# Storing the two fp32r parts of x column-block-major for the expert gather's weight loads

## The reference, cut to what matters

```python
x = layer_norm(ALPHA * x + h, ln1_g[i], ln1_b[i])
m = moe_ffn(x, router_w[i], router_bias[i], exp_w1[i], exp_w3[i], exp_w2[i], sh_w1[i], sh_w3[i], sh_w2[i])
x = layer_norm(ALPHA * x + m, ln2_g[i], ln2_b[i])
...
def step(out, args):            # one expert, inside moe_ffn
    tok, g, e = args
    xe = xpad[tok]              # the tokens of this expert: the gather
    h = jax.nn.silu(xe @ w1[e]) * (xe @ w3[e])
    y = (h @ w2[e]) * g[:, None].astype(xe.dtype)
    return out.at[tok].add(y), None
```

## Time and profile before

| | us |
|---|---|
| median of 3 runs | 1493.35 (1493.33 to 1494.79) |
| the profiled execution | 1495.15 |
| its span in the profile | 1493.4 |
| PE busy | 1432.8 (96%) |
| PEld busy | 900.3 (60%) |
| DVE, ACT, POOL busy | 508.3, 356.5, 50.2 |
| share of the chain that ended last | PE 91%, DVE 5%, ACT 2% |
| HBM traffic | 308 GB/s over the span, 400 to 420 GB/s in the expert loops |

### The profile page before, as it was taken

The page is one execution under the profiler, slowest core; times in us unless marked ns, Lnnn a source line. Parts: engine busy times, 40 slices in busy tenths (PEclk is TensorE's granted clock), DMA queues, the critical chain, the costliest instruction groups (busy, mean ns, idle before and its releaser), DMA issues.

```text
span 1493.4 us, 21684 instructions
## 1 busy us (share of the span) xinstructions
PE 1432.8 (96%) x8704; PEld 900.3 (60%) x8704; DVE 508.3 (34%) x840; ACT 356.5 (24%) x878; POOL 50.2 (3%) x75
## 2 busy tenths in 40 slices
PE   8978999999999999999899999999999999999988
PEld 3467586566565656654478476765666656565543
DVE  0397261332323223232610346222323322232253
ACT  1137132222222222221210242222222222222211
POOL 1220010000000000000100001000000000000000
PEclk9969999999999999999899999999999999999999
DMA  9530147999999999998564504499999999999951
GB/s 308 181 148 1 74 178 322 400 416 407 413 414 412 411 405 414 408 418 343 166 213 145 225 2 169 174 420 411 400 409 414 410 421 405 413 404 409 421 211 56
DMA packets 80807, 461.89 MB, mean 309 GB/s; under 512 B 9168, under 2 KB 9392, under 8 KB 30544
## 3 DMA queue, kind: packets, MB, share of 16 engines
q1 hardware_dynamic: 78128, 452.07, 75.1%
q0 software_dynamic: 2592, 8.53, 1.9%
HBM read 459.52 MB, written 1.05 MB: 308 GB/s over the span
## 4 chain that ended last, share of the span: by engine, by line
PE 91%; DVE 5%; ACT 2%; issue 1%; DMA 0%; SPq 0%; DVEq 0%
PE ps L907 30%; PE ps L935 15%; PE ps L877 10%; PE ps L949 9%; PE ps L1053 4%; PE ps L794 4%; PE ps L749 3%; PE ps L634 3%; PE ps L766 2%; PE ps L818 2%; PE ps L590 1%; PE ps L917 1%; PE ps L619 1%; PE ps L513 1%; PE ps L734 1%; PE ps L827 1%
## 5 line engine op out<-in xcount | busy, mean ns | idle before, releaser
L1681 DVE TENSOR_TENSOR o_tok<-ps,o_tok 128x1024 f32<-128x1024 f32 x128 | 156.6, 1224 | 347.0 <-PE ps L949 347.0
L935 PE MATMUL ps<-ring,qkT 128*64 128x512 f32 x1024 | 233.8, 598 | 1.2 <-ACT qkT L1228 1.2
L907 PE MATMUL ps<-ring,proj 128*64 128x256 f32 x2048 | 228.1, 381 | 0.0
L907 PEld LDWEIGHTS ps<-ring,proj 128*64 128x64 f32 x2048 | 144.2, 137 | 80.8 <-issue 11.5
L935 PEld LDWEIGHTS ps<-ring,qkT 128*64 128x64 f32 x1024 | 68.2, 136 | 133.3 <-issue 133.3
L1673 DVE SCALAR_TENSOR_TENSOR roped<-roped,rows,ps 128x256 f32<-128x256 f32 x64 | 30.7, 480 | 316.1 <-ACT roped L1222 316.1
L1249 ACT ACTIVATE y_hi<-ps 128x1024 fp32r<-128x1024 f32 x64 | 65.6, 1024 | 293.4 <-PE ps L949 287.4
L907 PE MATMUL ps<-ring,pT 128*64 128x256 f32 x1024 | 123.1, 382 | 2.2 <-ACT gb_row L1216 2.2
L907 PE MATMUL ps<-ring,gb_row 128*64 128x256 f32 x1024 | 121.5, 379 | 0.0
L877 PE MATMUL ps<-sel,x_hi 128*128 128x512 f32 x256 | 118.2, 462 | 0.0
L949 PE MATMUL ps<-y_hi,selT 128*128 128x512 f32 x256 | 112.5, 439 | 4.0 <-DVE y_lo L1687 4.0
(11 more groups left out here) (248 smaller groups left out, 1404.3 us busy)
## 6 DMA issues: line engine op xcount, KB each, us to landing
ring<-in_exp_w_dram SPq DMA_DIRECT2D x384, 1024.0 KB, 10.9
ring<-in_od_w_in_dram SPq DMA_DIRECT2D x6, 2048.0 KB, 8.5
ring<-in_ple_w_gate_dram SPq DMA_DIRECT2D x4, 2048.0 KB, 10.4
ring<-in_ev_w_in_dram SPq DMA_DIRECT2D x3, 2048.0 KB, 21.2
ring<-in_sh_w_dram SPq DMA_DIRECT2D x6, 1024.0 KB, 6.9
ring<-in_ev_w_o_dram SPq DMA_DIRECT2D x2, 2048.0 KB, 11.0
ring<-in_od_w_o_dram SPq DMA_DIRECT2D x2, 2048.0 KB, 8.4
ring<-in_ev_w_in_dram SPq DMA_DIRECT2D x2, 1024.0 KB, 9.9
```

The source lines that it names most:

```text
L907: ins = pe.matmul(ps[b * SLOTS:(b + 1) * SLOTS, 2, w * FE:(w + 1) * FE], xe(odd, c)[:, u * P + b * SLOTS:u * P + (b + 1) * SLOTS], views[b ...
L935: ins = pe.matmul(ps[b * SLOTS:(b + 1) * SLOTS, 4 + half, :], hT[:, f, b * SLOTS:(b + 1) * SLOTS], views[b][:, f, half * PIECE:(half + 1) ...
L1681: dve.tensor_tensor(y_acc[:, t, :], ps[:, bank:bank + 2, :].rearrange("p b n -> p (b n)"), y_acc[:, t, :], ALU.add)\
```

## The change

In the expert gather nothing is computed differently. POOL now writes both parts in the order c n (chunk, then row) instead of n c, so element n of chunk c lies at c times 128 + n. It still reads `x_tok` in its own order, so its writes step by 512 bytes between neighbours (inner run of 8), and in the subtraction the second operand is read with that step too. The weights of a gather matmul become 128 neighbouring elements. No instruction is added, removed or moved on any engine, and no wait; only access patterns change. The counts stay: on POOL 4 of L481, 4 of L482 and 4 of L485, on PE 512 matmuls of L877, each with its weight load. Where the diff adds lines, later line numbers grow by up to 3.

```diff
                 for t in range(NT):
                     pool.wait_ge(sem(f"ln1_out{L}"), t + 1)
-                    step(pool.tensor_copy(x_lo[:, t, :], x_tok[:, t, :]))
-                    step(pool.tensor_tensor(x_lo[:, t, :], x_tok[:, t, :], x_lo[:, t, :], ALU.subtract))
+                    lo = x_lo[:, t, :].rearrange("p (c n) -> p n c", c=DC)
+                    x_t = x_tok[:, t, :].rearrange("p (n c) -> p n c", c=DC)
+                    step(pool.tensor_copy(lo, x_t))
+                    step(pool.tensor_tensor(lo, x_t, lo, ALU.subtract))
                 pool.wait_ge(sem("shared_up"), NT * (L + 1))
                 for t in range(NT):
-                    pool.tensor_copy(x_hi[:, t, :], x_tok[:, t, :]).then_inc(sem("x_split"), 1)
+                    pool.tensor_copy(x_hi[:, t, :].rearrange("p (c n) -> p n c", c=DC),
+                                     x_tok[:, t, :].rearrange("p (n c) -> p n c", c=DC)).then_inc(sem("x_split"), 1)
...
                             for part in (x_hi, x_lo):
-                                ins = pe.matmul(ps[:, bank + c, :], part[:, t, 2 * j + c::DC], sel[:, t, :],
+                                ins = pe.matmul(ps[:, bank + c, :], part[:, t, (2 * j + c) * P:(2 * j + c + 1) * P], sel[:, t, :],
                                                 start=(t == 0 and part is x_hi), stop=(t == NT - 1 and part is x_lo))
```

## The result

The changed kernel takes 1481.45 us (median of 4 runs, 1480.87 to 1481.77) against 1493.39 us before (4 runs, 1493.33 to 1494.79). The ratio is 0.9924, 95% interval 0.9912 to 0.9937: 0.8% faster, 11.9 us. Forecast were 1480.4 us in a range of 1476.5 to 1487.

The account below looks back on a forecast made before the run. PE, with 91% of the last-ending chain, was taken as the bound. Weight loads -13.6 us and POOL +0.6 us gave -13.0 us, from 1493.35 to 1480.4 us, in a range of 1476.5 to 1487.

Parts of the forecast that it names:

- PE as the bound: Expert loop: PE carries 91% of the last-ending chain, so a nanosecond off PE there is one off the end.
- Weight loads: Expert gathers: matmul distances become the scatter's; 12.7 us from 56 gathers in steps, 0.9 from octet 0, 13.6 us off PE.
- The shorter inner distance: Rival, expert gather: distance between its matmuls falls to 0.22 us or less, 20 to 22 us gained, 1473 us; chance 0.05.
- POOL: Casts and subtraction with 512-byte write step: up to about 1.1 us longer; half taken, once, +0.6 us.
- the prediction's signs of being wrong: Loads above 250 ns, gather above 2.1 us, ring waits in octet 7, PE waiting for x_split or the router's gates.
- the wait that I forecast: Layer 2 norm: longer first POOL subtraction holds DVE, lengthening PE's 1.63 us wait; paid in full, +0.6 us.
- the router's cover: Layer 1: last gate step ends at 206.85, PE wants it at 210.85; 4.0 us hide the second subtraction's delay.
- The queue: Expert weight DMA: follows steps of 15.12 us at 416 GB/s, since it moved 422; last pair has 0.5 us less time.
- Queue as the bound: Rival, expert steps: queue no faster than before, PE waits in last steps; 6.9 us gained, 1486.4 us; chance 0.09.
- head only: Rival, expert gather: only the first distance shortens, inner ones stay at 0.244 us; -9.3 + 0.6 us, 1484.7; chance 0.08.
- no effect: Rival, gather weight loads: stay at 0.33 us, only POOL's 0.6 us remains, 1494 us; chance 0.04.
- The slower rival: POOL's strided subtraction sets the layer's start; decides from about 3.4 times its time, 1499 us at 4 times; chance 0.03.

Follow-up runs that it names:

- E1: Kernel before with only the gather's reads side by side, POOL's writes as before (result differs from the reference); 1479.49 us, ratio 0.990.
- E2: Changed kernel with the gather's reads back at the 32-byte step, POOL writing the new order (result differs from the reference); 1494.63 us, ratio 1.0008.
- E4: The change with four chunks interleaved instead, so weights lie 16 bytes apart and POOL writes runs of four; 1489.48 us, ratio 0.9975 to the kernel before.
- E6: Kernel before with only x_lo stored and read in the new order, x_hi as before; 1489.42 us, ratio 0.9977.
- E3: The change with two chunks interleaved instead, so weights lie 8 bytes apart and POOL writes pairs; 1479.72 us, ratio 0.9894 to the kernel before.
- E5: Kernel before with only x_hi stored and read in the new order, x_lo as before; 1484.64 us, ratio 0.9945.
- E10: E3 (8-byte order) run again; 1482.8 us, ratio 0.993 to the kernel before.
- E9: The changed kernel run again, on the chip of E10 and E11; 1480.64 us, ratio 0.9911 to the kernel before.
- E8: Changed kernel whose gather leaves out x_lo, 4 matmuls instead of 8; 1464.65 us, ratio 0.9797 to the kernel before.
- E11: E3 with the subtraction moved from POOL to DVE, behind the router's gates; 1479.75 us, ratio 0.9904 to the kernel before.

## Why the prediction was right

**PE as the bound.** Right. The saved time of the gathers, 11.8 + 1.0 = 12.8 us, arrived: the two stretches from first gather to last `exp_up` fell by 13.0 us and the span by 13.5. The 0.5 us between them, against a cost of 0.5 us on POOL's account, lie outside the expert loops and are within what the stretches at 1.2 GHz move.

**Weight loads.** The mechanism was right in both halves: the 32-byte step makes the loads long (E1, E2), and they are paid at the head and hardly inside (E4 to E6). The term of 13.6 us measured 12.8 to 13.0. In its parts: the head gave 0.13 us where 0.16 was taken from the scatter (perhaps since the gather follows a matmul of another shape, which no run tests); the inner distances gave 0.011 us each where 0.009 was taken. The two runs of 32 gave as much as counted (1.0 against 0.9 us), but by another way: their own head is 0.64 us before and after (214.61 to 215.25), and the 31 inner distances brought it all.

**The shorter inner distance.** Inside a gather of the changed kernel the distance is 0.233 us and in its runs of 32 it is (222.33 - 215.25) / 31 = 0.228. Neither reaches 0.22, so the rival of 20 to 22 us fell. Nor does any reach the 216 ns of the Trainium skill (TensorE: Matmul & The Clock Gate, "Back-to-back issue gap"). The prediction used that figure for a stream; the section gives it for a matmul by itself, and about 131 ns for a stream of loads and matmuls, which no stream of these runs comes near. The 107 ns of its section "LDWEIGHTS" are not met either: 187 and 188 ns side by side.

**POOL.** The size came out (+0.6 us forecast; measured 1.80 - 1.28 = 0.5 us in the change's own profile and 0.34 + 1.78 - 1.75 = 0.4 in E1 and E2), but its place was wrong, so the size was luck. The wait for the router's gates stood among the prediction's signs of being wrong. I let the longer subtraction lengthen PE's wait for the norm. In fact that wait vanished, because the subtraction of layer 2 began later than the norm's L1439, after 11.39 us in which POOL waited for nothing that the profile shows. This gap is 9.3 to 9.9 us in all profiles with the old or nearly old cast of `x_lo` (before, E1, E3, E4, E5, E10) and 11.2 to 11.7 us in all with the longer one (E2, E6 to E9); why it exists and why it grows stays open. Tenths of a us decide what is paid. In E8 it is 11.21 us, the subtraction starts together with the norm's L1455, and PE waits for the norm after all, 2.98 us, and not for the gates:

```profile
901.45 2.85 POOL L484 TENSOR_TENSOR x_lo<-x_tok,x_lo 128x1024 fp32r<-128x1024 f32 x1 [11.21 <-issue]
901.45 3.92 DVE L1455 SCALAR_TENSOR_TENSOR x_tok<-x_tok,rows,gb_row 128x1024 f32<-128x1024 f32 x1
905.49 1.97 PE L516 MATMUL ps<-const,x_tok 128*128 128x128 f32 x8 [2.98 <-DVEq L1456]
```

That is the wait that I forecast, at 2.98 - 1.63 = 1.35 us instead of 0.6. In the change itself the cost came at the gates: the work on `x_lo` took away the router's cover (E6), and the casts of `x_hi`, which I had counted as covered by 4.8 us, did the rest. They delay no reader, but while they ran DVE's L1610 stood for 3.75 us. The cover was counted for the reader of the result and not for the engine that POOL holds up. Per instruction: a cast costs 0.9 to 1.0 us more (the estimate from PE's load was 1.1), a subtraction 0.5 us more.

**The queue.** Right that it could follow, and the reason was the right one: 422 GB/s with a backlog, confirmed by E8 at 421. I had expected 0.5 us less time from issue to use at the last pair; it stayed at 19.96 us, since `exp_up` and the steps of octet 7 did not change. What moved is the landing, 1.0 us later in layer 1 and 0.2 us earlier in layer 2.

**The rivals.** Queue as the bound, head only, no effect: each is excluded by a number of the profile after (no wait ahead of L910, 0.233 us, 187 ns). The slower rival needed POOL at 3.4 times its time; its subtraction takes 1.2 times as long and its casts 1.9 to 2 times.

## What to carry to other kernels

Compare a stream's start-to-start distance with that of a like stream elsewhere in the trace, not the durations: 0.14 us longer loads cost 0.13 us only at the head of each burst and 0.01 us inside. For fp32r weights keep the step at 8 bytes or less; side by side brings 5 ns a load more, which no median here can tell, and interleaving pairs leaves the writer nearly as fast as it was. Where POOL gets a longer instruction, look for what DVE does at that time, not only for who needs the result.

## What the runs showed of the hardware beyond that

POOL's one-input cast holds DVE up too: with 3.76 us of casts L1610 took 3.75 us for 64 columns instead of 0.19. In E9 the same casts held two instructions, for 1.96 and 1.81 us. It goes both ways: in E11 a cast of `x_hi` beside DVE's subtraction took 2.1 us instead of 1.09, and that subtraction 2.11 us instead of 1.37.

PE all but hides even a long weight load behind a 512-column fp32r matmul: distances of 0.233 us with loads of 188 ns, 0.237 with 310 ns, 0.244 with 330 ns.

The short stretches at 1.2 GHz fall differently in each execution of one kernel. In the profile after, L821 in layer 1 fell into one and took 9.28 us for 64 matmuls, in layer 2 it took 7.76; before, a stretch fell into layer 2, where 32 of these matmuls took 5.18 us instead of 3.93. In E8, where PE waits for the queue, they also fall into the expert loops. This moves single executions by 1 to 2 us and sets how small a difference the medians can tell.
